# State space block: the two state buffers laid out with the time step as the inner index

## What is computed

```python
def s5_scan(u, a_re, a_im, log_dt, b_re, b_im, c_re, c_im, d_skip):
    uf = u.astype(f).reshape(B, S, SSM_N_GROUPS, SSM_GROUP)      # 64 groups of 16 channels
    a_bar = jnp.exp(A * dt)                                      # 64 complex states in each group
    bu = jnp.einsum('bsgc,gpc->bsgp', uf.astype(jnp.complex64), b_bar)
    _, states = lax.associative_scan(combine, (a_elems, bu), axis=1)
    y = jnp.einsum('bsgp,gcp->bsgc', states, Cm).real
    y = y + d_skip.astype(f).reshape(SSM_N_GROUPS, SSM_GROUP) * uf
    return y.reshape(B, S, SSM_WIDTH).astype(u.dtype)

def s5_mixer(h, w_in, ...):
    proj = h @ w_in
    u, z = proj[..., :SSM_WIDTH], proj[..., SSM_WIDTH:]
    y = s5_scan(u, ...)
    g = jax.nn.gelu(y)
    y = g * jax.nn.sigmoid(g @ w_glu + b_glu)
    return (y * jax.nn.silu(z)) @ w_out
```

## Time and profile before

| | |
|---|---|
| median of 3 runs | 3222.98 us (3219.58 to 3223.21) |
| the profiled execution | 3222.22 us, its span 3220.4 us |
| mean granted TensorE clock | 0.997 of full speed |
| busy: PE / DVE / ACT / POOL | 3156.3 / 1433.0 / 1255.0 / 805.0 us |
| scan on VectorE | 1406.71 to 1553.73 us |
| outputs on TensorE | 1555.52 to 1607.14 us |

### The profile page before, as it was taken

How to read it: one execution, slowest core, us unless ns; L and a number is a source line. 1 busy time by engine, 2 the same in 40 slices (tenths; PEclk the granted TensorE clock), 3 DMA queues, 4 the chain that set the end, 5 groups by cost and what they waited for, 6 DMA issues and landing times.

```text
span 3220.4 us, 48521 instructions
## 1 busy us (share of the span) xinstructions
PE 3156.3 (98%) x19411; PEld 2561.4 (80%) x19411; DVE 1433.0 (44%) x3305; ACT 1255.0 (39%) x2582; POOL 805.0 (25%) x407
## 2 busy tenths in 40 slices
PE   7999999999999998999999999999999999999999
PEld 6877778787887876777888888877788788877787
DVE  3342122221213125569333446554546845564566
ACT  4444444443443334412322433255343433354342
POOL 2155455111111124223154111100223111111231
PEclk9999999999999999999999999999999999999999
DMA  6113323143523233323354311111003332111113
GB/s 194 45 48 86 80 64 85 52 127 117 154 90 90 93 94 105 118 73 105 139 182 151 97 42 44 44 34 32 27 21 117 105 81 49 45 39 32 33 41 143
DMA packets 314342, 267.26 MB, mean 83 GB/s; under 512 B 63365, under 2 KB 276697, under 8 KB 314122
## 3 DMA queue, kind: packets, MB, share of 16 engines
q1 hardware_dynamic: 198970, 133.71, 14.7%
q10 hardware_dynamic: 115152, 130.49, 13.2%
HBM read 220.87 MB, written 48.58 MB: 84 GB/s over the span
## 4 chain that ended last, share of the span: by engine, by line
PE 52%; DVE 4%; ACT 2%; issue 2%; DMA 1%; ACTq 0%; POOL 0%; DVEq 0%; SPq 0%; POOLq 0%
PE psum L1493 25%; PE psum L383 8%; PE psum L308 5%; PE psum L1627 2%; PE psum L1607 2%; PE psum L1616 2%; PE psum L3097 1%; PE psum L1530 1%; DVE act_lo L2520 1%; PE psum L1520 1%; PE psum L3088 1%; PE psum L3072 0%; PE psum L1536 0%; PE psum L1563 0%; DVE arena L2282 0%
## 5 line engine op out<-in xcount | busy, mean ns | idle before, releaser
L2700 POOL TENSOR_TENSOR w_lo<-w_raw,w_hi 128x1024 fp32r<-128x1024 f32 x122 | 296.4, 2429 | 1481.2 <-ACT w_hi L3178 768.3
L1493 PE MATMUL psum<-act_hi,w_hi 128*128 128x512 f32 (+1 forms) x1376 | 513.0, 373 | 5.1 <-DVE act_lo L456 3.3
L2870 PE MATMUL psum<-act_hi,w_hi 128*128 128x512 f32 x1280 | 505.6, 395 | 4.8 <-ACT arena L1191 3.9
L2870 PE MATMUL psum<-act_lo,w_hi 128*128 128x512 f32 x1280 | 507.7, 397 | 0.0
L1493 PE MATMUL psum<-act_lo,w_hi 128*128 128x512 f32 (+1 forms) x1376 | 504.4, 367 | 0.0
L2870 PE MATMUL psum<-act_hi,w_lo 128*128 128x512 f32 x1280 | 504.2, 394 | 0.0
L1493 PE MATMUL psum<-act_hi,w_lo 128*128 128x512 f32 (+1 forms) x1376 | 504.1, 366 | 0.0
L3651 DVE CUSTOM_DVE_ANT_0 arena<-psum,arena 128x128 f32<-128x128 f32 (+1 forms) x384 | 112.1, 348 | 479.9 <-PE psum L2909 332.7
L1493 PEld LDWEIGHTS psum<-act_hi,w_hi 128*128 128x128 f32 x1376 | 260.6, 189 | 58.0 <-issue 15.0
L1493 PEld LDWEIGHTS psum<-act_hi,w_lo 128*128 128x128 f32 x1376 | 260.4, 189 | 44.8 <-issue 5.0
L1493 PEld LDWEIGHTS psum<-act_lo,w_hi 128*128 128x128 f32 x1376 | 260.9, 190 | 42.3 <-issue 5.5
(11 more groups left out here) (402 smaller groups left out, 5391.4 us busy)
## 6 DMA issues: line engine op xcount, KB each, us to landing
w_raw<-in_attn_w_in SPq DMA_DIRECT2D x80, 512.0 KB, 3.8
w_raw<-in_w_in SPq DMA_DIRECT2D x64, 512.0 KB, 4.0
spare<-in_w_mod ACTq DMA_DIRECT2D x24, 1024.0 KB, 7.8
x<-arena ACTq DMA_DIRECT2D x24, 512.0 KB, 2.9
arena<-weight_rows ACTq DMA_DIRECT2D x16, 512.0 KB, 6.7
w_raw<-in_ssm_w_in SPq DMA_DIRECT2D x16, 512.0 KB, 3.7
arena<-mc_mat ACTq DMA_DIRECT2D x16, 512.0 KB, 3.6
arena<-x ACTq DMA_DIRECT2D x16, 512.0 KB, 5.5
```

Of the source, the lines that this page charges most:

```text
L1493: ins = nc.tensor.matmul(psum[:, n % 2, 0:c], w[:, slot % 2, k * P:(k + 1) * P], a[:, k, c0:c0 + c], start=(m == 0), stop=(m == 23))
L2700: G.tensor_tensor(w_lo[:, par], w_raw[:, par], w_hi[:, par].bitcast(F32), ALU.subtract).then_inc(slot_split, 1)
L2870: ins = nc.tensor.matmul(psum[:, h % 2, :], w[:, (3 + j) % 2, k * P:(k + 1) * P], a[:, k, c:c + 512], start=(m == 0), stop=(m == 23))
```

## The change

One line: each state buffer is declared with the time step as its last (inner) index, and then viewed with its indices in the old order, so that no other line changes.

```diff
-        ST = [region(8192 + 4128 * h, 129, 2, GH) for h in range(2)]
+        ST = [region(8192 + 4128 * h, 2, GH, 129).rearrange("p r g t -> p t r g") for h in range(2)]
```

## The result

The changed kernel takes 3237.82 us, the median of 7 runs (3234.27 to 3248.68), against 3219.58 us (3217.68 to 3223.21, 7 runs) for the kernel before, run beside it: a ratio of 1.0062 [1.0048, 1.0077], slower by 18.2 us at the medians. A ratio in this text is worked out over the single times of both kernels, with its 95% interval, and so isn't quite the ratio of the two medians. The prediction was 3243 us, within 3232 to 3258, and slower by more than 0.2%.

The account below looks back on a forecast made before the run. TensorE was taken to bound the kernel, with VectorE's longer scan making it wait: scan 147.0 + 49.0 + 3.6 us from 1406.3, then outputs 19.9 + 1.7, ending 20.4 us later. Forecast 3243 us, range 3232 to 3258.

Parts of the forecast that it names:

- The race: State space outputs: TensorE reaches its wait at 1571.6, the scan ends at 1605.9, TensorE stands still for 34 us.
- over 30 us: Sign of being right: TensorE waits over 30 us for VectorE's L3856 ahead of half 1's outputs.
- Part 1, weight loads: Carried matmuls' state loads on TensorE: sixteen take 0.96 us instead of 1.84, 7.2 us less in each half.
- The two bounds: Weight-load gain for each of 16 pairs of group pairs: nothing at least, 1.1 us at most; 0.9 taken.
- rival of weights that don't become faster: Weight loads gain nothing, half 1's outputs take 27.1 us, time is 3250 us; chance 5%.
- Part 2, copies: ScalarE's copies L3830 and L3439 write contiguously: 0.4 us gained in half 0, 0.8 in half 1.
- Part 3, the scan: VectorE's scan pays 0.77 or 0.88 ns more for each spaced number, growing by 49.0 us.
- The twelfth split: GpSimd weight-tile split that the longer scan also meets, slowing VectorE: 3.6 us more.
- The rival of no price: Distance costs VectorE nothing, scan ends at 1553.3 before TensorE asks, 15.6 us gained, 3207 us; chance 7%.
- The clock: TensorE's granted clock is lower after the gap ahead of half 1's outputs: 1.7 us, added once.
- the predicted 1627.5: End of the state space outputs: scan end 1605.9 + 19.9 + 1.7, 20.4 us later than before.

Follow-up runs that it names:

- runs with one half each: Only one half's state buffer has time as inner index, the other as in the kernel before; ratios 1.0005 (half 0) and 0.9983 (half 1).
- run with half 1's scan cut short: Changed kernel without half 1's 28 scan operations on 480 numbers, output not right; 3209.44 us, ratio 0.9959 to the kernel before.
- the parts inside: Layout with real and imaginary part side by side, time steps 8 bytes apart, against the kernel before; 3209.8 us, ratio 0.9963.
- steps of 16 bytes: Layout with runs of four adjacent numbers, time steps 16 bytes apart, swapped product in two operations, against the kernel before; 3227.09 us, ratio 1.0013.
- run with 272 transposes: Changed kernel with 272 unread transposes on TensorE ahead of its wait for the scan; 3235.95 us, ratio 1.0054 to the kernel before.
- half 1 alone: Only half 1's state buffer has time as inner index, half 0's as in the kernel before; 3216.93 us, ratio 0.9983.
- run with 245 transposes: Changed kernel with 245 unread transposes on TensorE ahead of its wait for the scan; 3237.31 us, ratio 1.004 to the kernel before.
- half 0 alone: Only half 0's state buffer has time as inner index, half 1's as in the kernel before; 3222.7 us, ratio 1.0005.

## Why the prediction was right

**The race.** The prediction said that TensorE would reach its wait earlier and then stand still until the scan's end, so that half 0's gain would be lost. That is what the wait of 29.1 us shows. It was shorter than the 34 predicted, because TensorE came to it at 1574.8 instead of 1571.6 (half 0's outputs began at 1556.7 instead of 1554.3 and took 18.1 us instead of 17.3) and the scan ended at 1603.9 instead of 1605.9. That is just under the "over 30 us" that the prediction had named as its sign. The runs with one half each show the rule behind it: the same 173 us of scan cost 6.2 us of waiting in one and 0.3 in the other.

**Part 1, weight loads.** Sixteen in 0.97 us; 0.96 was worked out from L1520's pace. Right. The two bounds and the rival of weights that don't become faster are out. Half 1's outputs took 22.0 us, against 19.9 + 1.7 = 21.6.

**Part 2, copies.** L3439 takes 0.587 us, 0.47 less, a little more than the 0.42 expected by L3446. L3830 takes 0.69 where it had taken 1.03. Right in kind, and too small to be found in the end.

**Part 3, the scan.** A step on 480 numbers was to take 1.03 to 1.08 us and takes 1.05 to 1.06; 256 numbers were to take 0.65 and take 0.635. On 256 numbers that is (635 - 426) / 256 = 0.82 ns a number for reading and writing, where 0.88 was carried over from 16 and 256 bytes. The scan took 195.8 us and not 199.6. Put together from undisturbed operations it was about 4 x (30 x 0.425 + 14 x 0.66 + 14 x 0.19) = 98.6 us before. Now it is 4 x (30 x 0.632 + 14 x 0.21) + 28 x 1.05 + 28 x 1.02 = 145.6, since the 28 operations on 480 numbers of half 1 ran while TensorE stood still and took 1.02 on average. That is 47.0 more, where the prediction had 49.0. The measured growth is 48.8, which leaves 1.8 us, not 3.6, for what the splits add. The twelfth split does fall into the scan, beside these operations in the chain of waits of the changed kernel:

```profile
1555.41 2.38 DVE arena L3856
1557.81 2.45 DVE arena L3853
```

Together they take 3.6 us more than twice 0.63, so its own price is as predicted. With some 8 us for the small gaps between 232 operations, the twelve splits took (195.8 - 145.6 - 8) / 12 = 3.52 us each, and the eleven of before (147.0 - 98.6 - 8) / 11 = 3.67: on average each is a little cheaper beside the longer operations. This is an estimate, and no run isolates it. So of the 3.8 us the pace accounts for 2.0 and the splits for 1.8.

**The rival of no price**, at 3207 us, was the strongest on the other side. The Trainium skill's rule in VectorE: DVE Perf Modes, section "Mode 1× (REGULAR) — the baseline", would have brought it. It doesn't hold for this kernel: 635 against 426 ns for the same count of float32 numbers, and all that differs is where they lie. The run with half 1's scan cut short shows that the arithmetic of that rival was near: without the wait for VectorE, 12.8 us are gained of the 15.6.

**Why 516 bytes cost what 16 do.** The prediction carried the price over from 16 and 256 bytes and couldn't say why. The runs with the parts inside and with steps of 16 bytes bracket it. At 8 bytes VectorE's split product and its copies (0.69 us) pay nothing, the weight loads next to nothing (193 ns against 188) and ScalarE's copies little (0.643 us on average against 0.587 contiguous and 1.06). At 16 bytes the copies and the weight loads pay in full, and so did the product that reads one operand so the earlier trace rows. The limit lies between; past it the distance hardly matters, up to the 516 bytes measured. The Trainium skill gives a rule that fits in Advanced Engine Details and Errata, section "Memory Cachelines": SBUF has cachelines of 16 bytes, and a line needs at least two hits to hide its access latency. The figures at 8 and 16 bytes agree with it. What goes on in the memory no run here shows.

**The clock.** The prediction added 1.7 us once. The run with 272 transposes shows this term: behind the wait the chain of the changed kernel has 1.22, 2.01 and 1.28 us where the same passes take 0.71, 1.09 and 1.09 elsewhere, 1.6 us more, and with the gap filled the first of them run at full pace.

**The rest.** The outputs ended 1.6 us ahead of the predicted 1627.5: the scan started 1.8 us later (the clock's slow stretches in the layer ahead fell otherwise in this profile: one of 13.7 us near 1225 us that the profile of before doesn't have, while two of 3.4 us that it has are missing), took 3.8 less, and half 1's outputs 0.4 more. That the first two nearly cancel is luck. Of the 5.2 us between the forecast of 3243 us and the median, some 3 lie in the kernel before, whose median was 3222.98 in the first 3 runs and 3219.58 in the 7 beside the changed kernel; the forecast shift was 20.4 us and the measured one 18.2. The shift at the outputs' end of the two profiled executions, 18.7 us, is close to that. The two profiled executions differ by 23.2; another 4.5 us came later. One piece of them is a second stretch at the lower clock near 1631 us, in the transposes right behind the block (windows of the changed kernel):

```profile
1631.00:1634.50 3.50, 3.49 (x12) 2.81 (x13) 3.50 (x4) 2.56 (x3) 3.50 (x2) 0.56 1.04 421
```

At 0.56 this stretch cost about 3.5 x 0.44 = 1.5 us. The kernel before has the same small gaps there and no slow stretch. When the same TensorE instructions are matched in both traces, 0.8 us more come bit by bit up to 2491 us of the trace of before, and the last 2.1 between 2491 and 2593 us, where each trace has two short stretches at the lower clock. What brings them isn't settled. The seven times of the changed kernel go with their mean clock: four at 0.993 took 3234 to 3238 us, two at 0.990 took 3244 and 3245 (the profiled one among them), and one at 0.988 took 3249. So the profiled execution carries more time at the lower clock than the median one, and the 23.2 us are not all the change's.

## What to carry to other kernels

Where two engines share a buffer and want different inner indices, look for the smallest unit that satisfies both: here two adjacent float32 numbers (8 bytes) for VectorE and a step of 8 bytes for the weight load, which kept the scan at its contiguous pace and the load within 5 ns of its own, and made the kernel 12 us faster than before. Price a layout on every engine that touches it, and then ask for each who waits for it: 48.8 us more on VectorE had 26 us of slack, some 14 us less on TensorE lay half ahead of the wait, where it was lost, and half behind it, where it counted. When a change fails on such a race, try its part behind the wait alone; half 1 alone gained 5 us of the same change that lost 18 as a whole.

## What the runs showed that had not been expected

- The price of spacing is a step and not a slope. 8 bytes: 193 ns for a weight load (188 contiguous). 16 bytes: 326. 128 bytes: 308. The load at 16 bytes is even the slowest.
- VectorE's spaced operations depend on what TensorE does. In the run with 245 transposes, VectorE's timeline around their end at 1604.6 us:

```profile
1602.41 1.06 DVE L3859 TENSOR_TENSOR arena<-arena 128x480 f32<-128x480 f32 x1
1603.51 1.05 DVE L3856 TENSOR_TENSOR arena<-arena 128x480 f32<-128x480 f32 x1
1604.60 1.00 DVE L3857 TENSOR_TENSOR arena<-arena 128x480 f32<-128x480 f32 x1
1605.63 1.01 DVE L3858 TENSOR_TENSOR arena<-arena 128x480 f32<-128x480 f32 x1
```

  The change comes at the moment TensorE stops. In the changed kernel itself such operations, with no GpSimd split beside them, take 1.03 to 1.08 while TensorE works and 1.00 to 1.03 while it waits. With 272 transposes in the place of that wait the same 28 operations take 1.02 to 1.06.
- What a TensorE gap cost behind it did not grow steadily with its length. After gaps of 3.2, 6.2 (half 0 alone), 14.6 and 29.1 us the first direct, carried and direct passes took 1.4, 1.5, 2.2 and 1.6 us more than elsewhere. The gap of the earlier trace rows was shorter still: TensorE was idle for 1.9 of its 2.6 us, and the clock was at 0.65 and 0.53 in the 4.2 us behind it.
- The loads of `mc_mat` became the next wait as soon as the outputs ran faster: 1.5 us with three buffers, 0.2 with four. The prediction had held them hidden, by 3.6 us for a load against 4.3 between two; in the profile of the changed kernel the page gives a median landing of 4.1 us.
